# Third attention of a three-layer kernel: value products in fp32r with paired query blocks, normalisation on GpSimd

## What is computed

```python
# q: 8 heads of 64; keys and values: 2 groups, each for 4 heads
for each block of 128 queries, each head:
    p_c = masked_softmax(q @ k_cmp.T * scale)      # 31 compressed keys
    p_s = masked_softmax(q @ k_sel.T * scale)      # causal
    p_w = masked_softmax(q @ k_win.T * scale)      # causal
    out = g0 * (p_c @ v_cmp) + g1 * (p_s @ v_sel) + g2 * (p_w @ v_win)
```

## Time and profile before

| | |
|---|---|
| time, median of 3 runs | 1905.97 us (1905.83 to 1909.02) |
| the profiled execution | 1907.46 us, of which its span 1905.7 us |
| PE busy | 1882.7 us, 99% |
| DVE / ACT / POOL busy | 879.4 / 795.8 / 950.7 us |
| mean granted clock of PE | 0.996 |
| third attention | 1281.1 to 1399.9 us |

### The profile page before, as it was taken

One profiled execution on the slowest core, in us unless ns is written; L12 is line 12 of the kernel. 1 busy time (PEld: TensorE's weight loads), 2 busy tenths in 40 slices (PEclk: granted clock), 3 DMA queues, 4 the chain that ended last, 5 costly groups with the idle time before them and its releaser, 6 DMA issues.

```text
span 1905.7 us, 26934 instructions
## 1 busy us (share of the span) xinstructions
PE 1882.7 (99%) x9217; PEld 1573.9 (83%) x9217; DVE 879.4 (46%) x1814; ACT 795.8 (42%) x1412; POOL 950.7 (50%) x1236
## 2 busy tenths in 40 slices
PE   9999999999999999999999999999999999999999
PEld 6878888888888888888888888888888888888887
DVE  6967642222336675422222673696643354444200
ACT  6558642323233576432222353636652333323221
POOL 6740265555546542554555564452135455555553
PEclk9999999999999999999999999999999999999999
DMA  6330133332322212333323323221113323233332
GB/s 221 113 103 2 40 100 100 95 96 96 100 90 92 74 45 66 97 99 100 99 89 99 100 79 98 67 78 45 34 56 100 100 80 108 89 103 94 110 100 78
DMA packets 47438, 168.30 MB, mean 88 GB/s; under 512 B 5616, under 2 KB 5872, under 8 KB 47088
## 3 DMA queue, kind: packets, MB, share of 16 engines
q1 hardware_dynamic: 46368, 164.64, 27.0%
q10 hardware_dynamic: 976, 2.39, 0.5%
HBM read 164.13 MB, written 2.10 MB: 87 GB/s over the span
## 4 chain that ended last, share of the span: by engine, by line
PE 91%; DVE 6%; ACT 1%; issue 1%; DMA 0%; SPq 0%; DVEq 0%; ACTq 0%
PE bank L611 26%; PE bank L613 26%; PE bank L612 26%; PE bank L727 4%; PE bank L695 3%; PE bank L712 2%; PE bank L772 1%; DVE KT L1419 0%; PE bank L869 0%; DVE KML L1447 0%; DMA X<-x 0%; PE bank L666 0%; PE bank L724 0%; PE bank L654 0%; PE bank L777 0%
## 5 line engine op out<-in xcount | busy, mean ns | idle before, releaser
L568 POOL TENSOR_TENSOR WL<-RAW,WH 128x256 fp32r<-128x256 f32 x1208 | 932.9, 804 | 924.3 <-ACT WH L973 924.1
L611 PE MATMUL bank<-XH,WH 128*128 128x512 f32 x1311 | 524.2, 400 | 4.3 <-DVE VN L1775 2.0
L613 PE MATMUL bank<-XH,WL 128*128 128x512 f32 x1311 | 512.0, 391 | 0.0
L612 PE MATMUL bank<-XL,WH 128*128 128x512 f32 x1311 | 511.4, 390 | 0.0
L973 ACT ACTIVATE WH<-RAW 128x1024 fp32r<-128x1024 f32 x302 | 316.6, 1051 | 301.4 <-PE bank L613 298.6
L611 PEld LDWEIGHTS bank<-XH,WH 128*128 128x128 f32 x1311 | 247.0, 188 | 54.7 <-DVE VN L1775 2.2
L613 PEld LDWEIGHTS bank<-XH,WL 128*128 128x128 f32 x1311 | 246.6, 188 | 52.2
L612 PEld LDWEIGHTS bank<-XL,WH 128*128 128x128 f32 x1311 | 247.1, 189 | 48.8 <-issue 1.9
L611 PE MATMUL bank<-HH,WH 128*128 128x512 f32 x512 | 199.2, 389 | 0.0
L612 PE MATMUL bank<-HL,WH 128*128 128x512 f32 x512 | 199.2, 389 | 0.0
L613 PE MATMUL bank<-HH,WL 128*128 128x512 f32 x512 | 199.2, 389 | 0.0
(11 more groups left out here) (377 smaller groups left out, 2769.6 us busy)
## 6 DMA issues: line engine op xcount, KB each, us to landing
RAW<-stream SPq DMA_DIRECT2D x302, 512.0 KB, 3.5
out<-X SPq DMA_DIRECT2D x8, 256.0 KB, 4.7
X<-x SPq DMA_DIRECT2D x3, 512.0 KB, 7.1
MEM<-mem SPq DMA_DIRECT2D x1, 1024.0 KB, 10.1
W<-cmp_w ACTq DMA_DIRECT2D x1, 1024.0 KB, 4.6
KT<-KR ACTq DMA_DIRECT2D x1, 768.0 KB, 7.0
CT<-consts SPq DMA_DIRECT2D x1, 513.0 KB, 11.3
X<-x SPq DMA_DIRECT2D x2, 256.0 KB, 3.2
```

The costliest lines, as they stand in the source:

```text
L568: ins = pool.tensor_tensor(WL[:, slot, c], RAW[:, slot, c], WH[:, slot, c].bitcast(F32), ALU.subtract)
L611: pe.matmul(dst, lhs[0], rhs[0], start=start, stop=False)
L612: pe.matmul(dst, lhs[0], rhs[1], start=False, stop=False)
L613: return pe.matmul(dst, lhs[1], rhs[0], start=False, stop=stop)
```

## The change

In the third attention alone:

- Values are kept as fp32r: ACT writes the rounded values into columns 0 to 63 of an operand, DVE the rest (value minus rounded value) into columns 64 to 127. One stationary operand so gives the product with the high values in output rows 0 to 63 and with the low ones in rows 64 to 127; they are added at the head's end.
- The turned probabilities are split in two parts: ACT's copy rounds to fp32r (PTH), DVE subtracts it from PSUM (PTL). The PSUM bank is free for the next turn after DVE's step.
- Units are reordered so that two query blocks of one branch follow each other, and value products are made once for a pair, with up to 256 columns, one product for PTH and one for PTL. They run in every second iteration, 8 iterations behind the scores. The compressed branch's product is made in two halves of 256 columns.
- POOL normalises the rows (64 steps), with six weight conversions placed between them.
- The rows of probabilities now go round six buffers; four small tiles move to a place of their own.

The core of the diff:

```diff
-TURN_LAG, VALUE_LAG = 5, 7
+TURN_LAG, VALUE_LAG = 5, {"mla": 7, "swa": 7, "nsa": 8}
+PAIRED = ("nsa",)
...
-                    VN = tensor(q_k_v, "VN", [P, NT, 2 * P])
+                    VN = tensor(q_k_v, "VN", [P, NT, 2, NG, 2 * HD], F32R)
...
+                for b0, br, second in itertools.product((0, 2), range(2), range(2)):
+                    b = b0 + second
+                    nk = (b + 1) * P
+                    units.append(Unit(
+                        stacked(QN[:, h, blk(b)], KNH[:, br, g, 0:nk], KNL[:, br, g, 0:nk]), nk, TRI[:, S - nk:S],
+                        [VN[:, kb, br, g, :] for kb in range(b + 1)], 0, blk(b0, 2), start=br == 0,
...
+        def pair_part(part, j, n):
+            return part[:, j // 2 % 2, 0:n, blk(j % 2)]
+
+        def pair_values(units, j):
+            first, second = units[j - 1], units[j]
+            for kb in range(second.nb) if second.start else reversed(range(second.nb)):
+                at = 0 if kb < first.nb else P
+                yield second.values[kb], slice(at, 2 * P), slice(second.out_cols.start + at, second.out_cols.stop), kb
...
 (POOL)
-            lo_parts(early, converted("merge"))
-            lo_parts(converted("merge"), plan.tiles)
+            lo_parts(early, plan.out_tile[plan.out0["gates"]] + 1)
+            for i, u in enumerate(units):
+                row, c = prob[i % len(prob)][:, u.keys], i % 8
+                pool.wait_ge(signal("nsa_summed"), i + 1)
+                pool.tensor_scalar(row, row, RS[:, c:c + 1], u.weight, ALU.mult, ALU.mult
+                                   ).then_inc(signal("nsa_prob"), 1)
+                if i % PER_GATE == 4 and i < 2 * EARLY_GATES * PER_GATE:
+                    n = plan.out_tile[plan.out0["gates"] + i // PER_GATE] + 1
+                    lo_part(n, n % RING)
+            lo_parts(plan.out_tile[plan.out0["merge"] - 1] + 2, plan.tiles)
...
 (PE)
-                            pe.wait_ge(signal(name + "_pt"), j - nt + 1)
+                            pe.wait_ge(signal(name + ("_pt_lo" if name in PAIRED else "_pt")), j - nt + 1)
...
+                    if 0 <= j and name in PAIRED and j % 2:
+                        pe.wait_ge(signal(name + "_pt_lo"), j + 1)
...
+                        for v, cols, out_cols, kb in pair_values(units, j):
+                            pe.matmul(bank[:, out_cols], v, PTH[:, j // 2 % 2, kb, cols], start=u.start and kb == 0,
+                                      stop=False)
+                            ins = pe.matmul(bank[:, out_cols], v, PTL[:, j // 2 % 2, kb, cols], start=False,
+                                            stop=not u.start and kb == 0)
...
 (ACT)
+                        if name in PAIRED:
+                            if j >= 4:
+                                act.wait_ge(signal(name + "_values"), j // 2 - 1)
+                            act.activation(pair_part(PTH, j, u.nb), bank[:, 0:u.nk].rearrange("p (a n) -> p a n", n=P),
+                                           ACT.Copy).then_inc(signal(name + "_pt"), 1)
...
+                act.wait_ge(products_done, plan.out_mark[o])
+                act.activation(VN[:, b, :, :, 0:HD], BANK[o % RING][:, 0:2 * P].rearrange("p (r g n) -> p r g n", r=2, g=NG),
+                               ACT.Copy, scale=RCOL[:, b:b + 1]).then_inc(signal("v_hi"), 1)
                 act.wait_ge(drained, o + 1)
                 act.activation(GATE[:, b, :], BANK[o % RING][:, 2 * P:2 * P + NGATE], ACT.Exp,
...
 (DVE)
+                    j = i - TURN_LAG - 1
+                    if name in PAIRED and 0 <= j < n:
+                        dve.wait_ge(signal(name + "_pt"), j + 1)
+                        dve.tensor_tensor(pair_part(PTL, j, u.nb),
+                                          BANK[TURNED[name][j % len(TURNED[name])]][:, 0:u.nk].rearrange("p (a n) -> p a n", n=P),
+                                          pair_part(PTH, j, u.nb).bitcast(F32), ALU.subtract
...
+                            own.then(dve.tensor_tensor(HEAD_LOW[0:HD, :], bank[0:HD, :], hi.bitcast(F32), ALU.subtract))
+                            dve.tensor_tensor(lo, bank[HD:P, :], HEAD_LOW[0:HD, :], ALU.add).then_inc(signal(name + "_lo"), 1)
...
-                            dve.tensor_scalar(VN[:, b, :], output(in2 + LAST_V - 3 + b)[:, 0:2 * P], RCOL[:, b:b + 1],
-                                              None, ALU.mult).then_inc(drained, 1)
+                            dve.wait_ge(signal("v_hi"), b + 1)
+                            dve.scalar_tensor_tensor(VN[:, b, :, :, HD:2 * HD], values, RCOL[:, b:b + 1],
+                                                     VN[:, b, :, :, 0:HD].bitcast(F32), ALU.mult, ALU.subtract
```

More of the change, by code:

```diff
@@ L286, in program @@
         UNUSED = tensor(ctx, "UNUSED", [P, 1])
+        W2 = tensor(ctx, "W2", [P, HD])
+        H1 = tensor(ctx, "H1", [P, 64])
+        PEW = tensor(ctx, "PEW", [P, 2, HD])
+        KB = tensor(ctx, "KB", [P, NG, 64])
         VAR, STD, RCOL, POSQ = SM[:, 0:4], SM[:, 4:8], SM[:, 8:12], SM[:, 12:16]
@@ L337, in program @@
         with ExitStack() as block2:
-            W1 = tensor(block2, "W1", [P, 16, 2, HD])
+            with ExitStack() as compression:
+                W1 = tensor(compression, "W1", [P, 16, 2, HD])
+            PTL = tensor(block2, "PTL", [P, 2, NT, 2 * P], F32R)
             YAH = tensor(block2, "YAH", [P, 4, S], F32R)
@@ L464, in nsa_units @@
                 g = h // (NH2 // NG)
[L465 to L474, removed]
+                for b0, br, second in itertools.product((0, 2), range(2), range(2)):
[4 more added lines that the diff above has]
+                        [VN[:, kb, br, g, :] for kb in range(b + 1)], 0, blk(b0, 2), start=br == 0,
+                        weight=GATE[:, b, 3 * h + 1 + br:3 * h + 2 + br],
+                        head_end=yb_tile(h) if b == NT - 1 and br == 1 else None))
             return units
@@ L676, in attention @@
                 n, ns, nt = len(units), len(SCORES[name]), len(TURNED[name])
-                for i in range(n + VALUE_LAG):
+                for i in range(n + VALUE_LAG[name]):
                     for step in meanwhile.get(i, []):
@@ L1021, in attention @@
                 n = len(units)
-                for i in range(n + VALUE_LAG + 1):
+                for i in range(n + VALUE_LAG[name] + 1):
                     if i in meanwhile:
@@ L1470, in attention @@
                 n = len(units)
-                for i in range(n + VALUE_LAG + 2):
+                for i in range(n + VALUE_LAG[name] + 2):
                     if i in meanwhile:
@@ L1493, in attention @@
                         dve.wait_ge(signal(name + "_exp"), i)
-                        own.step(dve.reciprocal(RS[:, c:c + 1], SUM[:, c:c + 1]))
-                    j = i - VALUE_LAG - 2
+                        if name in PAIRED:
+                            dve.reciprocal(RS[:, c:c + 1], SUM[:, c:c + 1]).then_inc(signal(name + "_summed"), 1)
+                        else:
+                            own.step(dve.reciprocal(RS[:, c:c + 1], SUM[:, c:c + 1]))
+                    j = i - VALUE_LAG[name] - 2
                     if j >= 0 and units[j].head_end:
```

64 lines of the change are left out of this document (38 added, 26 removed).

## The result

The changed kernel takes 1914.99 us (median of 5 runs, 1911.64 to 1916.34) where the kernel before takes 1905.97: a ratio of 1.0041, 95% interval 1.0030 to 1.0052. It is 0.4% slower. Timed once more at the end (e12), the ratio was 1.0039 (1.0025 to 1.0053). The forecast was 1898.5 us, the range 1892 to 1906.

A forecast was written before the change was run, and what follows sets the result against it. PE was taken to bound the third attention. The terms were -14.0 (products) + 1.65 (entrance) + 3.0 (iterations without gate) + 1.9 (end) = -7.45 us, giving a median of 1898.5 us; range 1892 to 1906.

The forecast's parts named there:

- Value products, -14.0 us: Third attention: f32 products removed (35.5 us), fp32r products added (21.5 us); PE gains 14.0 us, between 12.4 and 16.6.
- Compressed product: Third attention: 16 calls of 256 columns with half the rows stream as many columns; no gain and no loss.
- Iterations without a gate product, +3.0: Third attention: in these iterations PE waits for DVE's subtraction to free turned-row banks; +3.0 us, bounds 0 and 6.
- the end, +1.9: Third attention's last units: turns wait for subtractions and ACT's copies, nothing left to hide chains; +1.9 us, bounds 1 and 4.
- a sign of being wrong: Third attention: waits for the subtraction in iterations with gate products, where a 0.25 us margin was to prevent any.
- ACT's wait for the pair's values: Third attention: ACT's copy of an even unit waits for values of the pair two before; covered, so no cost.
- Entrance, +1.65: Start of third attention: DVE's low values wait for ACT's high copies, PE waits behind; +1.65 us, clock dip kept.
- GpSimd: Third attention: POOL's 64 normalisations take 0.41 to 0.73 us; with conversions 57 us of work, which fits without delaying PE.
- Rival (b): Third attention: hops 0.3 us longer than counted add 6.65 us of waits; 1905.2 us, no measurable change; chance 0.17.
- (a): Third attention: hand-overs between engines cost nothing; -13.35 us, 1892.6 us; chance 0.14.
- (c): Third attention: POOL's normalisations become the bound; at 1.45 us each the stage lasts 125 us, 1912 us; chance 0.08.
- (d): Third attention: PE's clock falls again, 1.8 us each time; a second stretch at the entrance gives 1900.3 us; chance 0.06.

The follow-up runs named there:

- e12: The changed kernel as it is, timed once more against the kernel before: 1913.55 us, ratio 1.0039.
- e3: Changed kernel with the compressed products taking all 128 columns of the stationary operand instead of 64 (output differs there): 1909.38 us, ratio 1.0011 to the kernel before.
- e2: Changed kernel with three banks for turned rows and two for scores: 1903.91 us, ratio 0.9984 to the kernel before.
- e4: Changed kernel with ACT copying both high values of a half before the gate exponentials at the entrance: 1910.76 us, ratio 1.0018 to the kernel before.
- e8: Kernel before, with only the change's POOL part added (POOL normalises rows, weight conversions between them): 1907.43 us, ratio 0.9999.
- e5: Changed kernel with compressed values zero-padded to 128 columns and one 512-column product per head instead of two halves: 1904.64 us, ratio 0.9981 to the kernel before.
- e11: Kernel before, with each compressed product split into two with 64 columns of the stationary operand each: 1909.55 us, ratio 1.0009.

## Why the prediction was wrong

The time was forecast to fall by 7.45 us and rose by 7.4 to 7.8: a miss of 15 us. Two steps failed above all: the loop over the two banks of turned rows, which was given 4.9 us of waits and took 11.5, and the compressed product, which was put at nothing and cost 3.7 us. The value products' gain was mis-sized beside them. By its own steps:

- **Value products, -14.0 us.** Right in kind, too large. Added were 24.8 us instead of 21.5: 1.9 us more for the 128 products of 256 columns, 1.4 for the 64 of 128. In mid-pair the 0.12 us held (0.118 for 32 PTH products between others of 256 columns). The first product behind a turn took 0.202 us to the next start, but had itself started only 0.031 us after that turn, so that the two together cost what they do in unbroken rows; this is 1.3 us of the 3.3 and no loss. One behind two small products took 0.171. The small ones came to 7.5 us instead of 6.1: two at a pair's end took 0.172 us, the row's 0.085 each, two behind the compressed product 0.275. So the miss is 2.0 us. The Trainium skill's figure (TensorE: Matmul & The Clock Gate, "LDWEIGHTS (loading the stationary operand)") makes the small ones 6.8 us by estimate, nearer to the 7.5 measured than the row's price; but the 0.172 us for two at a pair's end lie below the 0.21 that the same figure gives.
- **Compressed product, "no gain and no loss".** Wrong: as many columns are streamed, but the stationary operand became 64 columns wide. Its records took 2.3 us more, and the turns just ahead of it 1.4 us, as their next start came after 0.20 us instead of 0.11: 3.7 us. e3 gave 4.6 us of stage back by the width alone. The rows showed no narrow operand, so this needed bounds and got none.
- **Iterations without a gate product, +3.0, and the end, +1.9.** The mechanism was right, a loop over two banks of turned rows that closes at DVE's subtraction. What the arithmetic left out is what else stands in DVE's queue: it held bias, subtraction and hops, but not the eight head ends of now 1.4 us, of which the change adds half, nor the six gate drains of 0.67 us. Nine waits in mid-stage stand in iterations without a gate product, 3.6 us recorded and some 5.1 with what the records hide, where 3.0 were forecast; five stand in iterations with one, 1.9 and 2.7 us, where none was, which the prediction had named as a sign of being wrong. Four of these five and two of the nine stand behind a head's end. Together that is 5.5 us, with what the records hide 7.7; at the end 3.0 and 3.8. In all 11.5 us instead of 4.9. e2 took 9.7 us back.
- **ACT's wait for the pair's values, "nothing".** Borne out as far as the runs go: with three banks ACT still waits 25.4 us there and PE hardly at all.
- **Entrance, +1.65.** Right: PE's wait grew by 1.73 us (3.75 for the 3.6 foretold), and e4 showed the chain behind it. The clock was kept as it was, with bounds of 1.8 either way; by the mean granted clock the whole execution loses 1.3 to 2.5 us more, and how much of it at the entrance isn't known.
- **GpSimd.** Right. The normalisations took 0.45 to 0.55 us (128 columns, by buffer) to 0.77 (512) on average; forecast were 0.41 to 0.73, and e8 shows no cost:

```profile
L624 POOL TENSOR_SCALAR TURN<-TURN,SM,GATE 128x512 f32<-128x512 f32 x6 | 4.6, 772 | 3.9 <-DVE SM L1548 3.9
L624 POOL TENSOR_SCALAR ACC<-ACC,SM,GATE 128x128 f32<-128x128 f32 x6 | 2.7, 450 | 2.5 <-DVE SM L1548 2.5
```

The misses add up to 6.6 (waits) + 2.0 (value products) + 3.7 (compressed products) + 2.1 (clock, the estimate from e12) + 0.1 (entrance) = 14.5 of some 15 us. The stage bears out the two in the middle: PE's work there fell by 8.0 us, and 14.0 - 2.0 - 3.7 is 8.3. Rival (b), the hand-overs eat the gain, was the nearest; it had the right mechanism and gave 6.65 us, about what the waits missed, but for another reason (longer hops); what was missing was a rival for the product's width. Rivals (a) and (c) were wrong, (d) right in part.

## What to carry to other kernels

When a buffer gets a second reader, write down everything that the second reader's engine does between, the rare steps too, and compare the loop with the other engine's work in the poorest iteration; one more buffer of that ring was worth as much here (9.7 us) as the cheaper products saved. A rare step of the slower queue costs least where the other engine's iteration is long (e5). Keep the width of the stationary operand the same from product to product, and pad with zeros if need be: "as many streamed columns" is not "the same time". And check a price from a row by a sum over the whole iteration: at a seam between kinds a record can lose what its neighbour gains.

## What the runs showed of the hardware

- Going from a stationary operand of 128 columns to one of 64 or back costs 0.14 us (e3, by the stage) to 0.16 us (by the records) on average over both ways, in e11 at most 0.17; no weight load ran under a product across the change.
- Two 64-column operands on different halves, 512 f32 columns each, ran together in 1.00 us, against 0.86 for one of 128 columns (e11).
- The first fp32r product of 256 columns behind f32 turns is recorded 0.03 us after the last turn, and the next one 0.20 us later; inside rows the steps are 0.11 and 0.12 us. The seam costs nothing in sum.
- The clock's losses came as 1.7 or 2.6 us behind the same wait, or not at all, differently for the same kernel (the changed kernel and e12); a single profile's clock is no property of a kernel.
